# Four norms and the final one in two token halves, and the conditioning tile moved behind the last up tile

## The chip, the core and the metric

The kernel runs on one core of a Trainium2 chip. Its engines work side by side, each from its own instruction stream, and wait for each other on semaphores: TensorE (PE in the profile, with its weight loads as PEld), VectorE (DVE), ScalarE (ACT), GpSimd (POOL) and SyncE (SP), which issues most DMAs. The metric is the time of the whole program on the device in microseconds (us).

## The reference

Two transformer stacks of two layers each run one behind the other on 512 tokens of 1024 channels, in float32. What matters here is the shape of a layer (first stack; the second has the same frame, its mixer has other parts, and its first layer also carries 256 context tokens):

```python
cond = jax.nn.silu(c)
for layer in range(DEPTH):
    mod = (cond @ ada_w[layer] + ada_b[layer])[:, None, :]
    shift_m, scale_m, gate_m, shift_f, scale_f, gate_f = jnp.split(mod, 6, axis=-1)
    h = rmsnorm(x, norm_mix_g[layer]) * (1.0 + scale_m) + shift_m
    mixed = attention_head_groups(...) if layer % 2 == 0 else gated_deltanet(...)   # ends in @ w_out
    x = x + gate_m * mixed
    h = rmsnorm(x, norm_ffn_g[layer]) * (1.0 + scale_f) + shift_f
    x = x + gate_f * swiglu(h, ffn_w_in[layer], ffn_w_out[layer])
return rmsnorm(x, final_norm_g)
```

`swiglu` is silu(h @ gate) * (h @ up), then @ down, with 2816 hidden channels. The conditioning of the second stack has one vector for its tokens and one for its context.

## The kernel before

Activations lie as [128 channels, 8 chunks, tokens]: `X` holds the residual stream. Layers are 0 to 3. Each large product is made of three passes over rounded operands: every operand is split in a high part (rounded by ScalarE) and a low part (the rest, by a subtraction), and `pe_three` or `pe_three_pair` multiply high by high, high by low and low by high. Weights come in tiles through a ring of four slots (`ring`), in the order of `linear_plan()`; ScalarE rounds a tile (`round_tile`, 128x2048, L386), GpSimd or, for the context's passes, VectorE makes the low part (`rest_tile`, L398), two buffers in turn. A projection's tile is "own" if TensorE multiplies it.

The feed-forward part goes in two halves of the hidden channels: `up{layer}{pass}{half}` with 11 own tiles (48 matmuls of 512 columns each), then `down...` with 8 tiles (33 matmuls each), which VectorE adds to `X` with the gate (L794). Beside the up tiles of layers 0 to 2 lie the tiles of the next layer's conditioning matrix ("ada" tiles), one behind each own tile. VectorE multiplies such a tile by the conditioning vector, chunk after chunk in a chain of its own (`dve_ada_tile`, L916 and L919: eight operations for one vector, sixteen for two), and TensorE adds up the partitions with matmuls of one column (`pe_ada_tile`, L935). There are two vectors beside up100, up101 and up200, one beside up000, up001 and up201. A twelfth ada tile per half, `after_down...`, stands behind the down tiles: VectorE works on it at the seventh down tile, TensorE behind the eighth. `dve_ada_end` then forms the modulation (`MOD`, `GAIN`).

Norms: `act_square` squares each chunk of `X` (ScalarE), `pool_add` sums the chunks (GpSimd, L824), `pe_norm_sum` sums over partitions with a matrix of ones (L836), `act_rstd` makes the reciprocal root by Ln and Exp (L842, L843). Then chunk by chunk VectorE scales (`dve_scaled_chunk`, L870), ScalarE adds the shift and rounds to `H_HI` (L857), and VectorE makes `H_LO` (`dve_rest_chunk`, L877), on which TensorE waits chunk by chunk (`wait_normed`). In front of up000, up100 and up300 this follows an output projection of four tiles (`pe_out`, `dve_out`, `act_out`, `pool_out`; an out tile also has 48 matmuls; its residual add is L611), in front of gdn_in and of the final norm it follows a down projection. The first tile of gdn_in is split in halves `U_HI`, `U_LO` behind the norm's Exp (`round_halves`, L1875, and L1890).

The order on each engine is its program order:

```python
def dve_split_norm(dve, name, gain, shift):
    dve.wait_ge(sig("norm_rstd"), RSTD_NO[name])
    dve_scaled_chunk(dve, NORMED, 0, T, gain, 0)
    dve_scaled_chunk(dve, NORMED, 0, T, gain, 1)
    for k in range(DC):
        if k + 2 < DC:
            dve_scaled_chunk(dve, NORMED, 0, T, gain, k + 2)
        dve_rest_chunk(dve, NORMED, T, shift, k)
```

## Time and profile before

| | |
|---|---|
| runs | 3418.53 us median of 3 (3416.69 to 3419.86) |
| profiled execution | 3420.76 us, span 3419.0 us |
| TensorE | busy 3194.0 us, 93% of the span |
| VectorE, ScalarE, GpSimd | 49%, 35%, 38% |
| mean granted TensorE clock | 0.974 |

The span runs from the first to the last instruction. A row of a timeline gives start, duration, engine, line, operation, output and inputs, how many alike are merged (x3), and in brackets how long the engine had been idle and what released it. PEclk is the granted clock of TensorE: 1.00 is 2.4 GHz, 0.50 is 1.2 GHz.

### The profile page before, as it was taken

The numbers are of one execution on the slowest core, as the hardware profiler recorded it, in microseconds if no ns is written. First come the engines' busy times: TensorE is split into PE (matmuls) and PEld (weight loads), VectorE is DVE, ScalarE is ACT, GpSimd is POOL, SyncE is SP. The second block draws the span as 40 slices with busy tenths as digits, with TensorE's granted clock in tenths as the row PEclk, the third lists the DMA queues.
The fourth block names the chain that finished last, engine by engine and source line by source line (L and its number), as shares of the span: only waits on it lengthen the run. The fifth ranks groups of instructions, "written<-read, shape, count | busy, mean of one in ns | idle before, by whom it ended". The sixth has DMA issues, their size and how long they took to land. (4 is left out here: it accounts for less than half of the span.)

```text
span 3419.0 us, 42414 instructions
## 1 busy us (share of the span) xinstructions
PE 3194.0 (93%) x16184; PEld 2510.1 (73%) x16184; DVE 1674.1 (49%) x2845; ACT 1180.5 (35%) x1519; POOL 1315.1 (38%) x719
## 2 busy tenths in 40 slices
PE   8998999998988899998988998999999997989998
PEld 7864788877768688886873367888899783378887
DVE  5534342426676574754836626634355738421111
ACT  3244322224744322223234432222444324432222
POOL 3314444344452433343315543344400424554443
PEclk9999999999999899999998999999999998999999
DMA  7510343432200243442110022444454211022321
GB/s 276 206 41 25 111 185 141 181 132 74 74 13 14 98 172 141 162 152 74 62 48 34 1 78 107 164 154 169 146 180 160 87 50 44 25 86 83 111 84 67
DMA packets 55219, 360.10 MB, mean 105 GB/s; under 512 B 5920, under 2 KB 6944, under 8 KB 19616
## 3 DMA queue, kind: packets, MB, share of 16 engines
q1 hardware_dynamic: 54208, 348.63, 27.8%
q10 hardware_dynamic: 864, 9.44, 0.7%
q8 instruction: 100, 1.64, 0.2%
q14 instruction: 47, 0.39, 0.0%
HBM read 355.95 MB, written 2.10 MB: 105 GB/s over the span
## 5 line engine op out<-in xcount | busy, mean ns | idle before, releaser
L398 POOL TENSOR_TENSOR W_LO<-ring,W_HI 128x2048 fp32r<-128x2048 f32 (+1 forms) x177 | 728.9, 4118 | 1052.5 <-ACT W_HI L386 1052.5
L454 PE MATMUL PS<-H_HI,W_HI 128*128 128x512 f32 (+1 forms) x1888 | 712.5, 377 | 29.7 <-DVE H_LO L877 23.0
L456 PE MATMUL PS<-H_HI,W_LO 128*128 128x512 f32 (+1 forms) x1888 | 703.0, 372 | 0.0
L455 PE MATMUL PS<-H_LO,W_HI 128*128 128x512 f32 (+1 forms) x1888 | 702.4, 372 | 0.0
L386 ACT ACTIVATE W_HI<-ring 128x2048 fp32r<-128x2048 f32 (+1 forms) x214 | 366.3, 1712 | 458.7 <-PE PS L444 417.8
L454 PEld LDWEIGHTS PS<-H_HI,W_HI 128*128 128x128 f32 x1888 | 359.5, 190 | 93.9 <-issue 32.0
L456 PEld LDWEIGHTS PS<-H_HI,W_LO 128*128 128x128 f32 x1888 | 358.7, 190 | 63.1
L455 PEld LDWEIGHTS PS<-H_LO,W_HI 128*128 128x128 f32 x1888 | 359.5, 190 | 59.2 <-issue 0.2
L919 DVE SCALAR_TENSOR_TENSOR PS<-ring,SC,PS 128x256 f32<-128x256 f32 x774 | 379.1, 490 | 27.2
L442 PE MATMUL PS<-HID_HI,W_HI 128*128 128x512 f32 (+1 forms) x880 | 325.3, 370 | 4.8 <-DVE W_LO L398 4.0
L444 PE MATMUL PS<-HID_HI,W_LO 128*128 128x512 f32 (+1 forms) x880 | 323.8, 368 | 0.0
L443 PE MATMUL PS<-HID_LO,W_HI 128*128 128x512 f32 (+1 forms) x880 | 323.7, 368 | 0.0
L650 ACT ACTIVATE GATED<-PS 128x512 f32<-128x512 f32 (+1 forms) x110 | 61.1, 555 | 725.0 <-PE PS L456 725.0
L665 DVE TENSOR_TENSOR HIDDEN<-GATED,PS 128x512 f32<-128x512 f32 (+1 forms) x110 | 69.7, 634 | 425.0 <-ACT GATED L650 425.0
L794 DVE SCALAR_TENSOR_TENSOR X<-PS,MOD,X 128x512 f32<-128x512 f32 (+1 forms) x80 | 55.7, 696 | 386.0 <-PE PS L444 386.0
L442 PE MATMUL PS<-H_HI,U_HI 128*128 128x512 f32 x520 | 208.3, 401 | 19.8 <-DVE H_LO L877 13.8
L443 PE MATMUL PS<-H_LO,U_HI 128*128 128x512 f32 x520 | 205.0, 394 | 0.0
L444 PE MATMUL PS<-H_HI,U_LO 128*128 128x512 f32 x520 | 204.5, 393 | 0.0
L442 PEld LDWEIGHTS PS<-HID_HI,W_HI 128*128 128x128 f32 x880 | 165.9, 189 | 34.5 <-DVE W_LO L398 5.3
L444 PEld LDWEIGHTS PS<-HID_HI,W_LO 128*128 128x128 f32 x880 | 165.9, 188 | 27.8
L443 PEld LDWEIGHTS PS<-HID_LO,W_HI 128*128 128x128 f32 x880 | 165.9, 189 | 27.0
L2596 POOL TENSOR_TENSOR U_LO<-ring,U_HI 128x1024 fp32r<-128x1024 f32 x40 | 102.5, 2564 | 214.7 <-ACT U_HI L2584 214.7
(401 smaller groups left out, 5315.3 us busy)
## 6 DMA issues: line engine op xcount, KB each, us to landing
ring<-w_tiles SPq DMA_DIRECT2D x271, 1024.0 KB, 4.8
ring<-d_tiles SPq DMA_DIRECT2D x80, 704.0 KB, 4.2
WORK<-bias_tables ACTq DMA_DIRECT2D x4, 1792.0 KB, 9.0
X<-xT SPq DMA_DIRECT2D x1, 2048.0 KB, 16.2
WORK<-rope_tables ACTq DMA_DIRECT2D x2, 1024.0 KB, 4.9
outT<-H SPq DMA_DIRECT2D x8, 256.0 KB, 2.2
X<-ctxT SPq DMA_DIRECT2D x1, 1024.0 KB, 9.0
CN<-consts SPq DMA_DIRECT2D x1, 835.0 KB, 7.2
```

What stands on the lines that cost most here:

```text
L386: act.activation(W_HI[:, b, 0:w], ring[:, g % SLOTS, 0:w], ACT.Copy).then_inc(sig("tile_rounded"), 1)
L398: eng.tensor_tensor(W_LO[:, b, 0:w], ring[:, g % SLOTS, 0:w], W_HI[:, b, 0:w].bitcast(F32), ALU.subtract).then_inc(sig("tile_split"), 1)
L442: pe.matmul(PS[:, o:o + w], hi(k), x_hi(k), start=k == 0, stop=False)
L443: pe.matmul(PS[:, o:o + w], hi(k), x_lo(k), start=False, stop=False)
L444: mm = pe.matmul(PS[:, o:o + w], lo(k), x_hi(k), start=False, stop=k == n - 1)
L454: pe.matmul(to, hi[:, cols(k, j)], x_hi(k), start=k == 0, stop=False)
L455: pe.matmul(to, hi[:, cols(k, j)], x_lo(k), start=False, stop=False)
L456: mm = pe.matmul(to, lo[:, cols(k, j)], x_hi(k), start=False, stop=k == n - 1)
L650: act.activation(GATED[:, v, 0:w], PS[:, v * 1024:v * 1024 + w], ACT.Silu).then_inc(sig("gate_silu"), 1)
L665: dve.tensor_tensor(HIDDEN[:, v, 0:w], GATED[:, v, 0:w], PS[:, v * 1024 + 512:v * 1024 + 512 + w], ALU.mult).then_inc(evac_done, 1)
L919: ins = dve.scalar_tensor_tensor(out=out, in0=w, scalar=c[:, k:k + 1], in1=acc, op0=ALU.mult, op1=ALU.add)
L2596: pool.tensor_tensor(U_LO[:, i % 2, :].rearrange("p (k c) -> p k c", k=DC), half_source(layer, t, j), U_HI[:, i % 2, :].rearrange("p (k c) ...
```

## The change

1. The norms in front of up000, gdn_in, up100 and up300 and the final norm work on two halves of the tokens (columns 0 to 255, 256 to 511). The last out tile (or last down tile) multiplies the first half for all its outputs, then the second; residual add, square, sum and reciprocal root of the last chunks are made per half. TensorE's sum of the first half lies inside the second half's matmuls, that of the second inside the first pair of the next projection (`pe_first_pair`), which is multiplied half by half.
2. In the up norms ScalarE rounds the second weight tile in four pieces (`round_second`) beside the second half's first chunks, and VectorE makes its low part in four pieces behind its last ones (`rest_second`). GpSimd, which made it before, waits for it.
3. In the last out tile ScalarE squares the tile before ahead of rounding the next weight tile, and GpSimd adds the squares ahead of the low part.
4. For gdn_in the first half weight tile is rounded in front of the norm's first half, the second inside it (`round_early`); the two halves lie in buffers of their own.
5. The twelfth conditioning tile is called `last_up...` and stands behind the last up tile. VectorE works on it behind the low part of the last hidden chunk; TensorE multiplies it inside the first down tile, in front of the last chunk. `dve_ada_end` comes at the third down tile.
6. The result is stored in pairs of chunks and token halves.

```diff
                     plan.append((up, "w", UP if layer == 3 else 2 * UP, UP, 1, None))
+                    if layer < 3:
+                        plan.append((f"last_{up}", "w", 1, 0, 1, None))
                     plan.append((down, "d", DC, DC, 1, None))
-                    if layer < 3:
-                        plan.append((f"after_{down}", "w", 1, 0, 1, None))
...
+        def pe_first_pair(pe, o, hi, lo, normed, between, ends, lag=(0, 0), second=None):
+            for h in range(2):
+                for s in range(DC + lag[h]):
+                    for j in range(2):
+                        k = s - lag[h] * j
+                        if not 0 <= k < DC:
+                            continue
+                        if j == 0:
+                            normed(h * DC + k)
+                        if j and k == h == 0 and second:
+                            second()
+                        to, x_hi, x_lo = PS[:, o + j * 512 + h * HALF:o + j * 512 + (h + 1) * HALF], H_HI[:, k, columns(h)], H_LO[:, k, columns(h)]
+                        pe.matmul(to, hi(j, k), x_hi, start=k == 0, stop=False)
+                        pe.matmul(to, hi(j, k), x_lo, start=False, stop=False)
+                        mm = pe.matmul(to, lo(j, k), x_hi, start=False, stop=k == DC - 1)
+                        if h and k == DC - 1 and ends[j] is not None:
+                            mm.then_inc(ends[j], 1)
+                    if h == 0 and s == 1:
+                        between()
...
+            b_p = base("act", "part_added", 2)
+            for j in range(2):
+                act.wait_ge(sig("part_added"), b_p + j + 1)
+                act_square(act, norm, 6 + j, 0, T)
+            act_rstd(act, norm, OUT_SUM, 0, T, chain, 0)
+            act_part(act, 0, 0, shift)
+            act_part(act, 0, 1, shift)
+            act.wait_ge(sig("out_first_added"), b + OWN[name])
+            act_square(act, norm, 8, 0, T)
+            for k in range(2, 5):
+                act_part(act, 0, k, shift)
+            act.wait_ge(evac_done, E0[name] + OWN[name])
+            act_square(act, norm, 9, 0, T)
+            act_part(act, 0, 5, shift)
+            act_part(act, 0, 6, shift)
+            act_rstd(act, norm, OUT_SUM, 0, T, chain, 1)
+            act_part(act, 0, 7, shift)
+            for k in range(DC):
+                if k < PIECES:
+                    round_second(act, norm, k)
+                act_part(act, 1, k, shift)
+            act.activation(SM[:, 45:46], SM[:, 1:2], ACT.Silu)
...
+            if halves:
+                next_own(pool, name, rest_tile, OWN[name] - 1, OWN[name] - 1, 0)
+                pool_add(pool, NEXT[name], DC, width)
...
+        def dve_norm_parts(dve, norm, gain, shift, between):
+            for h in range(2):
+                dve.wait_ge(sig("norm_rstd"), RSTD_NO[norm] - 1 + h)
+                for s in range(DC + 1):
+                    if s < DC:
+                        dve_part_scaled(dve, h, s, gain)
+                    if h == 0 and s + 1 in between:
+                        between[s + 1]()
+                    if s:
+                        dve_part_rest(dve, h, s - 1, shift)
+                    if h and s >= DC + 1 - PIECES and norm.startswith("up"):
+                        rest_second(dve, norm, s - (DC + 1 - PIECES))
...
                 dve.tensor_tensor(HID_LO[:, bass.ds(m, 1), 0:w], HIDDEN[:, v:v + 1, 0:w],
                                   HID_HI[:, bass.ds(m, 1), 0:w].bitcast(F32), ALU.subtract).then_inc(sig("hidden_split"), 1)
+                if "last_" + name in G0 and isinstance(m, int) and m == UP - 1:
+                    dve_ada_tile(dve, layer + 1, "last_" + name, int(name[-1]) * (UP + 1) + UP, 0, 0, 1, chain, apart=3)
...
+            def wait_first(k):
+                if k == UP - 1 and last in G0:
+                    pe_ada_tile(pe, layer + 1, int(name[-1]) * (UP + 1) + UP, 1, not closes(name))
+                wait_hidden(k)
...
                 next_own(dve, name, rest_tile, m, u, i)
-                if after in G0 and isinstance(m, int) and m == DC - 2:
-
-                    dve_ada_tile(dve, layer + 1, after, int(name[-1]) * (UP + 1) + UP, 0, 0, 1, chain)
...
+            shift = MOD[:, 1, 0:DC, 0]
+            for k in range(4):
+                act_part(act, 0, k, shift)
+            act.wait_ge(evac_done, E0[name] + DC)
+            act_square(act, norm, DC, 0, T)
+            round_early(act, 1)
+            act_part(act, 0, 4, shift)
+            act_part(act, 0, 5, shift)
+            act_rstd(act, norm, PART_SUM, 0, T, chain, 1)
...
+                    pe_first_pair(pe, 0, lambda j, k: U_HI[:, j, k * P:(k + 1) * P], lambda j, k: U_LO[:, j, k * P:(k + 1) * P],
+                                  normed, lambda: pe_norm_sum(pe, "gdn_in", PART_SUM, T, 1), (sig("half_done"), tile_done),
+                                  (4, 6), lambda: pe.wait_ge(sig("half_split"), 2))
...
-        def dve_out_norm(dve):
-            dve.wait_ge(sig("norm_rstd"), RSTD_NO["out"])
-            for k in range(DC):
-                dve.scalar_tensor_tensor(out=H[:, k, 0:T], in0=X[:, k, 0:T], scalar=FIN_G[1][:, k, 0:1],
-                                         in1=NORM_RSTD[:, 0:T], op0=ALU.mult, op1=ALU.mult).then_inc(sig("out_normed"), 1)
+        def dve_out_norm(dve, add_second):
+            for h in range(2):
+                dve.wait_ge(sig("norm_rstd"), RSTD_NO["out"] - 1 + h)
+                for k in range(DC):
+                    if h == 0 and k == 5:
+                        add_second()
+                    dve.scalar_tensor_tensor(out=H[:, k, columns(h)], in0=X[:, k, columns(h)], scalar=FIN_G[1][:, k, 0:1],
+                                             in1=NORM_RSTD[:, columns(h)], op0=ALU.mult, op1=ALU.mult).then_inc(sig("out_normed"), 1)
```

## Rows read from the trace of the kernel before

**Rows 1.** TensorE's waits: the row of the up projections' matmuls.

```profile
PE PS L454 <- DVE H_LO L877: 23.0, 5, 5.3
```

**Rows 2.** Timeline, norm before up300: start us, us, engine, line, operation.

```profile
3035.90 0.75 DVE L611 SCALAR_TENSOR_TENSOR X<-PS,MOD,X 128x512 f32<-128x512 f32 x1 [4.69 <-PE PS L444]
...
3039.91 2.08 DVE L870 SCALAR_TENSOR_TENSOR NORMED<-X,GAIN,NORM_RSTD 128x512 f32<-128x512 f32 x3 [3.26 <-ACT NORM_RSTD L843]
...
3042.79 0.47 PE L454 MATMUL PS<-H_HI,W_HI 128*128 128x512 f32 x1 [4.31 <-DVE H_LO L877]
...
3048.53 2.07 DVE L877 SCALAR_TENSOR_TENSOR H_LO<-NORMED,MOD,H_HI 128x512 fp32r<-128x512 f32 x3
...
3052.78 4.56 POOL L398 TENSOR_TENSOR W_LO<-ring,W_HI 128x2048 fp32r<-128x2048 f32 x1 [16.96 <-ACT W_HI L386]
...
3057.58 0.47 PE L454 MATMUL PS<-H_HI,W_HI 128*128 128x512 f32 x1 [2.03 <-POOL W_LO L398]
```

**Rows 3.** Windows, TensorE alone: busy time, instructions, granted clock.

```profile
core 0: us, PE busy (x), PEclk, DMA share, GB/s
370.00:380.00 10.00, 10.00 (x46) 1.00 0.19 62
2502.00:2507.00 5.00, 5.00 (x44) 1.00 0.42 144
1197.70:1203.50 5.80, 5.80 (x15) 0.51 0.75 280
3042.80:3048.00 5.20, 5.20 (x16) 0.67 0.00 0
3057.50:3063.50 6.00, 5.92 (x26) 1.00 0.49 175
```

**Rows 4.** Timeline, VectorE, the context's norm before layer 2.

```profile
1605.34 1.27 DVE L877 SCALAR_TENSOR_TENSOR CTX_LO<-BIG,MOD,CTX_HI 128x256 fp32r<-128x256 f32 x3
```

**Rows 5.** Timeline, norm before up000.

```profile
381.78 0.75 DVE L611 SCALAR_TENSOR_TENSOR X<-PS,MOD,X 128x512 f32<-128x512 f32 x1 [4.69 <-PE PS L444]
...
403.49 0.47 PE L454 MATMUL PS<-H_HI,W_HI 128*128 128x512 f32 x1 [0.60 <-POOL W_LO L398]
```

**Rows 6.** Timeline, norm before gdn_in.

```profile
763.49 0.75 DVE L794 SCALAR_TENSOR_TENSOR X<-PS,MOD,X 128x512 f32<-128x512 f32 x1 [6.73 <-PE PS L444]
...
768.49 5.47 POOL L1890 TENSOR_TENSOR U_LO<-ring,U_HI 128x1024 fp32r<-128x1024 f32 x2 [9.70 <-ACT U_HI L1875]
...
771.68 2.83 DVE L877 SCALAR_TENSOR_TENSOR H_LO<-NORMED,MOD,H_HI 128x512 fp32r<-128x512 f32 x1
...
774.65 0.77 PE L442 MATMUL PS<-H_HI,U_HI 128*128 128x512 f32 x1 [8.58 <-DVE H_LO L877]
...
784.78 2.40 POOL L1890 TENSOR_TENSOR U_LO<-ring,U_HI 128x1024 fp32r<-128x1024 f32 x1 [10.81 <-ACT U_HI L1885]
```

**Rows 7.** Timeline, up100's first conditioning tile.

```profile
1187.79 0.48 DVE L916 TENSOR_SCALAR PS<-ring,SC 128x256 f32<-128x256 f32 x1
...
1196.29 1.62 PE L935 MATMUL PS<-SM,ACC 128*128 128x1 f32 x8 [3.71 <-DVE ACC L919]
...
1197.77 0.77 PE L454 MATMUL PS<-H_HI,W_HI 128*128 128x512 f32 x1
```

**Rows 8.** Timeline, VectorE, the final norm.

```profile
3406.95 0.75 DVE L794 SCALAR_TENSOR_TENSOR X<-PS,MOD,X 128x512 f32<-128x512 f32 x1 [6.73 <-PE PS L444]
...
3410.96 5.39 DVE L1115 SCALAR_TENSOR_TENSOR H<-X,PR,NORM_RSTD 128x512 f32<-128x512 f32 x8 [3.26 <-ACT NORM_RSTD L843]
```

**Rows 9.** Timeline, VectorE, end of up100 and first down tile.

```profile
1308.96 0.69 DVE L668 TENSOR_TENSOR HID_LO<-HIDDEN,HID_HI 128x512 f32 x1 [0.95 <-ACT HID_HI L652]
...
1309.57 0.48 DVE L916 TENSOR_SCALAR PS<-ring,SC 128x256 f32<-128x256 f32 x1
...
1320.46 0.69 DVE L668 TENSOR_TENSOR HID_LO<-HIDDEN,HID_HI 128x512 fp32r<-128x512 f32 x1 [0.70 <-ACT HID_HI L652]
...
1326.88 0.75 DVE L794 SCALAR_TENSOR_TENSOR X<-PS,MOD,X 128x512 f32<-128x512 f32 x1 [5.73 <-PE PS L444]
```

More of the change, by code:

```diff
@@ L407, in over_own @@
             apart = SLOTS // per
-            rounds = (n - 1) // per
-            base = chain.n if chain else 0
+            rounds = (n - 1 - first) // per
             def step(m, v, i):
@@ L414, in step @@
                 body(m, v * apart, i)
+            for m in range(first):
+                step(m, m, 0)
+            base = chain.n if chain else 0
             if rounds:
@@ L554, in act_out @@
-            act_rstd(act, OUT_SUM, 0, width, chain)
+            if not in_halves_norm(norm):
+                squares(OWN[name] - 1)
+                act_rstd(act, norm, OUT_SUM, 0, width, chain)
+                return
+            b_p = base("act", "part_added", 2)
+            for j in range(2):
+                act.wait_ge(sig("part_added"), b_p + j + 1)
+                act_square(act, norm, 6 + j, 0, T)
+            act_rstd(act, norm, OUT_SUM, 0, T, chain, 0)
+            act_part(act, 0, 0, shift)
@@ L601, in dve_out @@
             b = base("dve", "out_first_done", OWN[name])
-            for m in range(OWN[name]):
+            for m in range(OWN[name] - halves):
                 for j in range(2):
@@ L816, in pool_add, with add @@
-        def pool_add(pool, k, w):
+                if m == 2 and last in G0:
+                    dve_ada_end(dve, layer + 1, last, chain)
+            if not halves:
+                dve_beside(dve, layer, name, DC - 1)
+                return
+            b_p = base("dve", "part_done", 1)
+            def add(h):
+                if h:
+                    dve.wait_ge(tile_done, g0 + DC)
+                else:
+                    dve.wait_ge(sig("part_done"), b_p + 1)
+                o = down_part(h)
+                dve.scalar_tensor_tensor(out=X[:, DC - 1, columns(h)], in0=PS[:, o:o + HALF], scalar=gate[:, DC - 1:DC],
+                                         in1=X[:, DC - 1, columns(h)], op0=ALU.mult, op1=ALU.add).then_inc(
+                    evac_done if h else sig("part_added"), 1)
@@ new lines, in dve_down, with in_halves_norm @@
+            add(0)
+            if norm == "out":
+                dve_out_norm(dve, lambda: add(1))
+            else:
+                dve_norm_parts(dve, norm, GAIN[:, 1, 0, :, 0], MOD[:, 1, 0:DC, 0], {4: lambda: add(1)})
+        CLOSED = {"down001": "gdn_in", "down101": "block", "down201": "in3", "down211": "in3_ctx", "down301": "out"}
+        IN_HALVES_NORM = {"up000": 2, "gdn_in": 1, "up100": 2, "up300": 2, "out": 1}
+        def in_halves_norm(norm):
+            return norm in IN_HALVES_NORM
@@ new lines, in square_units, with added_units @@
+        def square_units(norm):
+            cut = DC - IN_HALVES_NORM[norm] if norm in IN_HALVES_NORM else DC
+            return [(k, None) for k in range(cut)] + [(k, h) for h in range(2) for k in range(cut, DC)]
+        def added_units(norm):
+            return [n for n, (k, _) in enumerate(square_units(norm)) if 0 < k < DC - 1]
+        SQUARED_NO, ADDED_NO, SUMMED_NO, RSTD_NO = {}, {}, {}, {}
+        _at = [0, 0, 0, 0]
+        for _norm in ["attn_in", "up000", "gdn_in", "up100", "block", "in2", "up200", "in3", "in3_ctx", "up300", "out"]:
+            SQUARED_NO[_norm], ADDED_NO[_norm], SUMMED_NO[_norm] = _at[:3]
+            _parts = 2 if in_halves_norm(_norm) else 1
+            if _norm != "in2":
+                _at = [_at[0] + len(square_units(_norm)), _at[1] + len(added_units(_norm)), _at[2] + _parts, _at[3]]
+            _at[3] += _parts
+            RSTD_NO[_norm] = _at[3]
@@ L843, in act_rstd @@
             act.activation(r, r, ACT.Exp, scale=-0.5).then_inc(sig("norm_rstd"), 1)
-        RSTD_NO = {name: n + 1 for n, name in enumerate(
-            ["attn_in", "up000", "gdn_in", "up100", "block", "in2", "up200", "in3", "in3_ctx", "up300", "out"])}
         def act_split_norm(act, w, shift, silu=True):
```

364 lines of the change are left out of this document (257 added, 107 removed).

## The prediction

> **What bounds the kernel now.** I read the page first: TensorE is busy for 93% of the span, no other engine for more than half of it (the table above), so a change pays only where it takes away time in which TensorE waits or works slowly, and costs wherever it makes TensorE wait. Then TensorE's waits: the row at the top for the up projections names the low part of the normalised activations, 23.0 us in five waits [rows 1]. These waits are the ends of norms. Then the timeline around each of the five norms that the change halves, and the granted clock behind each stall.
>
> The norm in front of up300 shows the pattern [rows 2]. VectorE's last residual add (3035.90) follows the last matmul of the out projection by 0.2 us. Then sum of squares, Ln and Exp, and VectorE starts to scale at 3039.91; TensorE starts at 3042.79. VectorE's 16 operations end at 3050.60 (3048.53 and 2.07). Only then is the second weight tile rounded, GpSimd makes its low part from 3052.78 to 3057.34, and the second tile starts at 3057.58 after 2.03 us of waiting: 21.9 us after the out projection's last matmul (3035.70), for one tile of 48 matmuls. A tile costs 10.9 us at 0.227 us a matmul (46 in 10.00 us, less the overlap at the edges) [rows 3]. So nearly 9 us are lost here, two of them to a slow clock: behind the 4.31 us stall the clock is 1.2 GHz for some us. Granted clock in the rows: 0.67 over the 5.20 us behind that stall, 0.51 over 5.80 us from 1197.7, behind a stall of 3.71 us that comes up below, and 1.00 behind the one of 2.03 us [rows 3]. So 3.4 us (twice 0.33 of 5.20) to 5.7 us (twice 0.49 of 5.80) went at 1.2 GHz in place of 2.4, and half of it is lost: 1.7 to 2.9 us; I take 1.9 us.
>
> **The norm in front of an up projection, in halves (three places).** I count from the start of the last out tile, 10.9 us before its end; in this count VectorE now starts at 15.1, ends at 25.7, and the second tile starts at 32.8 [rows 2]. Matmuls of 256 columns follow each other by 0.1195 us (44 in 5.00 us, less the edges) [rows 3]; two make 0.239 us against 0.227 for one of 512, so halving costs 0.6 us a tile, and 4.8 us over the 402 matmuls halved (three out tiles, four first pairs, two down tiles). These are in the counts below. New order: first token half of the last tile done at 5.7, twelve matmuls of the other to 7.2, and the first half's add and square are done by then. The path from the add's start through square, sum, Ln and Exp to VectorE is 4.0 us now (3039.91 less 3035.90); what of it lies behind the square, at half width, I estimate at 2.2 us. VectorE starts at 9.4, 5.7 us sooner. A half operation repeats every 0.395 us (three from 1605.34 take 1.27, the last of them 0.48 on its own) [rows 4], so 32 take 12.6 us, where 16 whole ones take 10.6. It also gets two late residual adds (0.8) and four 512-wide pieces of the second weight tile's low part (such operations repeat every 0.66 us, 10.6 over 16; I take 0.6 for a plain subtraction): 15.9 us. Waits inside, all estimates: GpSimd's half add up to 0.7; the second half's Exp, which ScalarE takes behind parts 5 and 6, 0.9; and in the second half ScalarE rounds a 512-wide piece beside each of the first four chunks, 0.6 and 0.4 if it is as fast as VectorE by width, against VectorE's 0.79, so up to 1.0 more. VectorE ends at 28.1, **2.4 us later than now**. TensorE starts the first pair at 12.5, waits 0.9 for the last square, and ends with VectorE at 28.3. The wait is from the pieces: without inner waits VectorE ends at 25.3, with them doubled at 30.7. These are the bounds.
> - **up300** has no conditioning tiles. Second tile at 28.4 for 32.8: **-4.4 us** (-7.3 to -2).
> - **up000** has. VectorE makes the first conditioning tile behind the norm, and TensorE must multiply it before the second weight tile. Now this is hidden: second tile at 403.49, 21.9 us behind the last matmul's end (0.2 before 381.78), after 0.60 us for the weights [rows 5]. New: 28.1 and half of 8.3 (one vector) and 0.5: 32.8, the same; but TensorE has now stood for 4.2 us, so the clock falls: **+2.0 us** (-0.6 to +4.5).
> - **up100** has two vectors: 16 VectorE operations from 1187.79 until TensorE's 1196.29, 8.3 us of work and a little; TensorE already waits 3.71 us for them, and its second tile starts at 1197.77, 35.7 in this count, slow [rows 7]. VectorE 2.4 us later moves it by as much: **+2.3 us** (-0.4 to +4.8).
>
> **The norm in front of gdn_in.** The last residual add is at 763.49; GpSimd makes both low parts of the first weight tile from 768.49, 5.47 us, and VectorE's operation at 771.68 takes 2.83 us in place of 0.75; TensorE starts at 774.65, and the second weight tile is ready at 787.18 [rows 6]. From the last down tile's start (755.8) that is 31.5. New: first half of the tile to 4.0, twelve matmuls and sum to 6.5, VectorE from 7.5. The first low part comes before the norm; the second is made from 12.1 on, and holds VectorE by what the row at 771.68 shows, 2.83 less 0.75: 2.1 us. Chunk 4 is there at 15.1, TensorE waits 2.3 us for it, rest of the pair paced by VectorE to 23.5, then the trailing chunks, 27 matmuls: pair done at 26.7; the second tile's low part (2.40 us of GpSimd, started by the pair's first half at 23.9) is ready at 27.6: **-3.9 us** (-6, if nothing is held, to 0, if the clock falls in the pair and both holds are long).
>
> Here a rule of the Trainium skill bears on the case: SBUF — State Buffer, section "SBUF: two separate sides", says that a VectorE operation with two SBUF inputs and a GpSimd operation exclude each other for a whole instruction. By it the hold is all of GpSimd's operation, half of 5.47 us, and the pair ends 0.5 us later. The trace agrees (2.83 us at 771.68), and the sum above does not use it.
>
> **The final norm.** Add at 3406.95, eight operations from 3410.96 for 5.39 us, then the last store [rows 8]. From the last down tile's start (3399.3) VectorE now ends at 17.1. New: second half's reciprocal root at 12.8, eight half operations 3.2: 16.0. **-1.0 us** (-2 to +1: the stores have half as long runs, and nothing here shows their rate).
>
> **The conditioning tile behind the last up tile.** This is the largest term. Now VectorE makes it at the seventh down tile and TensorE multiplies it behind the eighth; neither waits. New: VectorE starts it behind the last low part of the hidden activations, and TensorE multiplies it inside the first down tile, before its last chunk. In order: that low part starts at 1320.46, and on the tile before VectorE's next operation starts 0.6 us after it (1309.57 after 1308.96), so 1321.1 here [rows 9]. Two vectors take 8.3 us, as above: ready at 1329.4. TensorE's last matmul of the first down tile ends 0.2 us before the add at 1326.88, and the last three start 0.7 before that: 1325.9 [rows 9]. It stands 3.5 to 3.6 us, with all eight down tiles queued in order behind it. Then eight tiny matmuls, and the clock falls, as at 1196.29 after 3.71 us: 1.9. **+5.5 us**, at each place with two vectors: behind up100, up101 and up200: **+16.5 us** (10.5 if the clock holds, 21 if each slow stretch is the longest). With one vector VectorE is ready at 1325.3 of this clock, some 0.3 us before TensorE asks (up000, up001, up201): 0. The multiplication itself only moves. The loads of the ring move by a slot; the first down tile's load is then released by the conditioning multiplication 11 us before its use, and rounding and low part (a larger tile's takes 4.56 us) still fit behind the load: 0, and about 1 us if they don't. SP's queue has nothing else behind it.
>
> Squares ahead of the next split, and the added order of waits, lie inside the last out tile beside TensorE's work: in the count above, 0 of their own.
>
> **Sum.** -4.4 + 2.0 + 2.3 - 3.9 - 1.0 + 16.5 = +11.5 us. The profiled execution took 3420.76 us, its span 3419.0; the median of the runs is 3418.53, 2.2 us below. From the median: **3430.0 us**.
>
> **Rivals.**
> - *No stall at the conditioning tile* (VectorE is ready by another order of its work than I read, so 16.5 falls to 0). For it: VectorE is idle half of the time on average. Against: the operations are a chain in program order, and up100 shows the same stall at 3.71 us. 3418.5 - 5.0 = 3413.5, no change by a hair. 0.08.
> - *Faster*: the stall as above is gone, or stays with the clock up (10.5), and the inner waits of the four half norms are absent, so that they stand at their low bounds: -7.3 - 0.6 - 0.4 - 6 - 2 = -16.3. With 10.5: 3412.7. It decides where VectorE needs no more than 15.9 us at an up norm. 0.10.
> - *Norms as computed or better, the stall short*: two of three stalls without a clock fall and up norms 1.5 us better each: about +2, 3421. 0.12.
> - *The hold of VectorE by GpSimd reaches the up norms.* GpSimd's low part of the first up tile (4.56 us) must now follow the first-half add and ends at 9.4, just as VectorE starts. 1 to 2 us late in each, and the clock falls in a first pair that stutters: +7 more, 3437. For it: the margin is nil. 0.12.
> - My forecast, its own range 3424 to 3436: 0.58.
>
> **Numbers.** Range: 3415 to 3439 leaves out some of the fast and of the slow rivals' tails. A measurement of this kernel tells some 0.2% (6.8 us) from no change. Slower by more (over 3425.4): 0.58 and 0.12, less a tail, 0.68. Within: 0.12, 0.08 and a hundredth of the forecast's: 0.21. Faster: 0.10 and a hundredth: 0.11.
>
> **What would show each step.** TensorE's waits: three rows at the conditioning multiplication of about 3.6 us inside the first down tiles of up100, up101, up200, and granted clock of half behind them. At up100 its wait for the conditioning tile grows from 3.7 to about 8 us; at up000 a new one of 4 us. The waits for the activations' low part shrink from 4.3 us to below 1 in the up norms, and at gdn_in to about 2.3. The spacing of halved matmuls stays 0.12 us. The prediction is wrong if VectorE ends an up norm near 25 in my count, or if its conditioning chain is ready before TensorE asks.

## The result and the profile after

The changed kernel took 3442.02 us (median of 4 runs, 3437.23 to 3444.36), the one before on the same chip 3419.2 us (4 runs, 3416.69 to 3424.51). The ratio is 1.0056, 95% interval 1.0044 to 1.0068: 19 us slower (15 to 23). Forecast were 3430.0 us, range 3415 to 3439, and slower with 0.68; so the sign is right and the size short by 8 us against the ratio. The profiled execution took 3444.36 us, span 3442.3, mean granted clock 0.967 (before 0.974); it is the slowest of the four, so its trace shows 23 us of loss where the ratio of the medians shows 19.

TensorE's waits after the change; the numbers behind a row are us in total, times, longest:

```profile
PE PS L1238 <- DVE ACC L1222: 36.4, 8, 11.2
...
PE PS L464 <- DVE H_LO L1180: 11.8, 2, 7.1
...
PE PS L497 <- DVE H_LO L774: 4.8, 9, 1.8
```

The waits for the activations' low part were 23.0 us in five [rows 1]. Of these two are left (11.8), in the whole norms at the very start (7.1, where it was 5.3) and before up200 (4.7); the three of 4.31 us in front of up000, up100 and up300 are gone, and small ones stand in the halved first pairs (L497). But the conditioning multiplication (L1238) waits 36.4 us in eight; before, it was 17.3 us in three. Of these 19 us, 9.9 are three new stalls at the moved tile, 3.7 a new one at up000, 4.2 the growth of the one at up100, and 1.3 small ones elsewhere. So the waits for the norms went down as forecast, and more came up on another row.

Timeline of the changed kernel at the end of up100 and the first tile of down100, VectorE and TensorE together (compare [rows 9]):

```profile
1322.16 0.69 DVE L852 TENSOR_TENSOR HID_LO<-HIDDEN,HID_HI 128x512 fp32r<-128x512 f32 x1 [0.70 <-ACT HID_HI L836]
1322.76 0.48 DVE L1219 TENSOR_SCALAR PS<-ring,SC 128x256 f32<-128x256 f32 x1
...
1327.47 0.39 PE L454 MATMUL PS<-HID_HI,W_LO 128*128 128x512 f32 x1
...
1330.63 0.48 DVE L1222 SCALAR_TENSOR_TENSOR ACC<-ring,SC,PS 128x256 f32<-128x256 f32 x1
...
1331.16 1.70 PE L1238 MATMUL PS<-SM,ACC 128*128 128x1 f32 x8 [3.31 <-DVE ACC L1222]
1332.72 0.77 PE L452 MATMUL PS<-HID_HI,W_HI 128*128 128x512 f32 x1
...
1334.38 0.75 DVE L1050 SCALAR_TENSOR_TENSOR X<-PS,MOD,X 128x512 f32<-128x512 f32 x1 [3.28 <-PE PS L454]
...
1343.78 0.75 DVE L1050 SCALAR_TENSOR_TENSOR X<-PS,MOD,X 128x512 f32<-128x512 f32 x1 [8.64 <-PE PS L454]
```

Read it from the bottom of the chain: the last of VectorE's sixteen operations ends at 1331.11, 8.35 us after the first began, and TensorE, which had stopped behind 1327.47, goes on at 1331.16. That is the predicted stall, 3.31 us for 3.5 to 3.6. The same row stands at 1529.05 (3.31) and 2239.09 (3.30), behind up101 and up200. Then the clock, in windows of TensorE alone (busy, matmuls, granted clock, DMA share, GB/s):

```profile
1320.00:1330.00 10.00, 7.86 (x39) 1.00 0.20 72
1331.00:1334.00 3.00, 2.84 (x11) 0.56 0.09 15
1334.00:1338.00 4.00, 4.00 (x11) 0.50 0.95 363
1338.00:1342.00 4.00, 4.00 (x19) 0.97 0.87 301
```

What a stretch loses is its length times what the clock lacks of 1.00: 0.44 of 3.00, 0.50 of 4.00, 0.03 of 4.00, together 3.4 us. The prediction had 1.9. Over the 8.00 us from 1529.00 and from 2239.00 the clock is 0.57 too, which gives 3.4 us each.

The conditioning waits at up000 and up100, the norm before gdn_in, and the norm before up300:

```profile
404.06 1.02 PE L1238 MATMUL PS<-SM,ACC 128*128 128x1 f32 x4 [3.69 <-DVE ACC L1222]
...
774.42 0.39 PE L497 MATMUL PS<-H_HI,U_PARTS 128*128 128x256 f32 x1 [1.83 <-DVE H_LO L774]
...
788.43 0.47 PE L452 MATMUL PS<-H_HI,U_PARTS 128*128 128x512 f32 x1 [1.53 <-POOL U_PARTS L2189]
...
1197.31 1.87 PE L1238 MATMUL PS<-SM,ACC 128*128 128x1 f32 x8 [7.88 <-DVE ACC L1222]
...
3054.96 0.28 PE L528 MATMUL PS<-O_HI,W_HI 128*128 128x256 f32 x1
...
3064.17 0.88 DVE L767 SCALAR_TENSOR_TENSOR HIDDEN<-X,GAIN,NORM_RSTD 128x256 f32<-128x256 f32 x2 [2.77 <-ACT NORM_RSTD L1150]
...
3081.41 0.69 DVE L659 TENSOR_TENSOR W_LO<-ring,W_HI 128x512 fp32r<-128x512 f32 x1
...
3082.36 0.40 PE L464 MATMUL PS<-H_HI,W_HI 128*128 128x512 f32 x1
```

At up300, counted from the last out tile's start (3054.96), VectorE starts at 9.2 (forecast 9.4), ends at 27.1 (28.1), and the second tile starts at 27.4 (28.4) where it was 32.8.

**Where the time went, stage by stage.** VectorE's residual adds mark the stages. The table gives the us from the first add of one projection to the first add of the next (to the end of the span in the last column), from the timelines of one profiled execution each; stages that never differ by more than 0.2 us are left out. The experiments' kernels are described below.

| kernel | out0 to down000 | down001 to out1 | out1 to down100 | to down101 | to out2 | out2 to down200 | to down201 | to down210 | down211 to out3 | out3 to down300 | down301 to end |
|---|---|---|---|---|---|---|---|---|---|---|---|
| before | 176.9 | 429.3 | 186.8 | 191.0 | 491.0 | 206.7 | 186.0 | 127.4 | 373.1 | 173.4 | 65.3 |
| act_peel | 176.9 | 430.2 | 185.1 | 191.0 | 494.6 | 206.8 | 186.1 | 124.6 | 375.4 | 173.4 | 65.3 |
| cond_only | 177.5 | 430.1 | 190.5 | 197.6 | 496.3 | 212.7 | 186.8 | 124.2 | 372.9 | 173.5 | 65.3 |
| **after** | 179.1 | 424.9 | 194.5 | 197.8 | 495.6 | 214.5 | 187.5 | 124.2 | 378.1 | 168.0 | 63.9 |
| filler | 179.3 | 428.3 | 191.6 | 194.6 | 494.9 | 211.5 | 185.6 | 124.2 | 379.8 | 168.0 | 64.0 |
| cond_short | 179.2 | 424.9 | 191.1 | 194.2 | 495.5 | 210.0 | 186.6 | 124.2 | 371.8 | 167.9 | 63.9 |
| cond_back | 179.3 | 428.2 | 187.3 | 191.1 | 496.0 | 207.1 | 186.5 | 124.2 | 379.9 | 168.0 | 63.9 |
| first_short | 177.5 | 423.9 | 185.8 | 191.1 | 494.1 | 208.7 | 186.5 | 124.2 | 378.0 | 168.0 | 64.0 |
| fill_first | 176.4 | 424.0 | 186.6 | 191.1 | 496.2 | 207.1 | 186.5 | 124.3 | 379.9 | 168.0 | 63.9 |
| up100_on | 177.5 | 423.2 | 188.2 | 191.0 | 494.8 | 206.7 | 186.5 | 124.2 | 376.6 | 167.9 | 64.0 |
| back_three | 177.5 | 423.2 | 185.2 | 190.9 | 494.6 | 206.8 | 186.5 | 124.2 | 380.1 | 167.9 | 63.9 |
| up300_off | 177.5 | 423.4 | 185.2 | 190.9 | 494.6 | 206.7 | 186.5 | 124.2 | 380.1 | 173.5 | 64.0 |

The columns of **after** add up to 21 us over before; the rest of the 23 us between the two spans is the stretch ahead of the first add (350.2 against 348.2).

### The profile page after: what moved, and what is told of

The parts are those of the page before. It is cut to its first block and busy times, and to the rows that moved or that the text cites. A ratio compares the mean times of both kernels' runs of the same rounds, so it can differ in the third digit from the quotient of the medians.

```text
span 3442.3 us, 43356 instructions
## 1 busy us (share of the span) xinstructions
PE 3217.5 (93%) x16606; PEld 2549.4 (74%) x16606; DVE 1702.1 (49%) x2937; ACT 1188.4 (35%) x1575; POOL 1301.5 (38%) x719
## 5 line engine op out<-in xcount | busy, mean ns | idle before, releaser
L406 POOL TENSOR_TENSOR W_LO<-ring,W_HI 128x2048 fp32r<-128x2048 f32 (+1 forms) x174 | 715.0, 4109 | 1075.2 <-ACT W_HI L394 1075.2
L464 PE MATMUL PS<-H_HI,W_HI 128*128 128x512 f32 (+1 forms) x1840 | 692.9, 377 | 13.0 <-DVE H_LO L1180 11.8
L466 PE MATMUL PS<-H_HI,W_LO 128*128 128x512 f32 (+1 forms) x1840 | 683.2, 371 | 0.0
L465 PE MATMUL PS<-H_LO,W_HI 128*128 128x512 f32 (+1 forms) x1840 | 683.2, 371 | 0.0
L464 PEld LDWEIGHTS PS<-H_HI,W_HI 128*128 128x128 f32 x1840 | 349.5, 190 | 72.3 <-issue 14.5
L466 PEld LDWEIGHTS PS<-H_HI,W_LO 128*128 128x128 f32 x1840 | 349.4, 190 | 61.0
L465 PEld LDWEIGHTS PS<-H_LO,W_HI 128*128 128x128 f32 x1840 | 349.9, 190 | 57.5 <-issue 0.2
L452 PE MATMUL PS<-H_HI,U_PARTS 128*128 128x512 f32 x504 | 202.6, 402 | 10.5 <-POOL U_PARTS L2189 5.6
L453 PE MATMUL PS<-H_LO,U_PARTS 128*128 128x512 f32 x504 | 199.5, 396 | 0.0
L454 PE MATMUL PS<-H_HI,U_PARTS 128*128 128x512 f32 x504 | 199.1, 395 | 0.0
L2901 POOL TENSOR_TENSOR U_PARTS<-ring,U_PARTS 128x1024 fp32r<-128x1024 f32 x40 | 102.6, 2566 | 217.1 <-ACT U_PARTS L2889 217.1
L454 PEld LDWEIGHTS PS<-HID_HI,W_LO 128*128 128x128 f32 x858 | 163.5, 191 | 27.6
```

The costliest lines, as they stand in the source:

```text
L406: eng.tensor_tensor(W_LO[:, b, 0:w], ring[:, g % SLOTS, 0:w], W_HI[:, b, 0:w].bitcast(F32), ALU.subtract).then_inc(sig("tile_split"), 1)
L452: pe.matmul(PS[:, o:o + w], hi(k), x_hi(k), start=k == 0, stop=False)
L453: pe.matmul(PS[:, o:o + w], hi(k), x_lo(k), start=False, stop=False)
L454: mm = pe.matmul(PS[:, o:o + w], lo(k), x_hi(k), start=False, stop=k == n - 1)
L464: pe.matmul(to, hi[:, cols(k, j)], x_hi(k), start=k == 0, stop=False)
L465: pe.matmul(to, hi[:, cols(k, j)], x_lo(k), start=False, stop=False)
```

## The experiments

Theory A: the loss is the conditioning tile with two vectors in the first down tile, by its stall and by the clock that falls behind it; the halved norms are a small gain in sum. Theory B: the loss comes from the halving itself (narrow matmuls, more instructions). Theory C: as A, but a stall costs only its length. Ratios are to the kernel before, which ran beside each. Where two ratios are compared, the difference carries some 5 us of uncertainty.

**cond_only.** Before, with the conditioning tile moved (part 5 of the change), and with the loops over own tiles (ScalarE's, and TensorE's in some down projections) in the changed form, that is, with their first step ahead of the loop:

```diff
+                    if layer < 3:
+                        plan.append((f"last_{up}", "w", 1, 0, 1, None))
                     plan.append((down, "d", DC, DC, 1, None))
-                    if layer < 3:
-                        plan.append((f"after_{down}", "w", 1, 0, 1, None))
```

> The kernel before with one part of the change alone: the conditioning tiles that stood behind the down tiles are made behind the last up tile and multiplied inside the first down tile; norms whole, as before. Theory A (the loss is here: at the three places with two vectors TensorE stands for VectorE's 16 operations, and its clock falls behind each): three waits of 3.3 us at the conditioning multiplication inside the first tiles of down100, down101 and down200, the stretch behind each at a lower granted clock, about 6.7 us a place, +20 us against before (3439). Theory B (the loss comes from the halved norms with their narrow matmuls and extra instructions, and the conditioning tile only moves): within 3 us of before. Theory C (the stalls cost only their length): +10 us.

Measured: 3442.94 us against 3423.18, ratio 1.0057 (1.0043 to 1.0072). That is 20 us (15 to 25) over before, with no norm halved; theory B falls. Theory C's +10 lies outside the interval, but the new form of the loops is in this kernel too, and alone it measured +3 us (0 to 6, act_peel below); the test of C by itself is filler. The three stalls are 3.31, 3.30 and 3.31 us. The slow stretch is not the same behind each: the granted clock is 0.57 over 8.00 us from 1328.50 and 0.79 over 8.00 us from 1526.30, so 3.4 and 1.7 us are lost there.

**cond_back.** The changed kernel, with the tiles of two vectors where they were:

```diff
-                    if layer < 3:
+                    one = layer == 0 or (layer == 2 and half == 1)
+                    if layer < 3 and one:
                         plan.append((f"last_{up}", "w", 1, 0, 1, None))
                     plan.append((down, "d", DC, DC, 1, None))
+                    if layer < 3 and not one:
+                        plan.append((f"after_{down}", "w", 1, 0, 1, None))
```

> The changed kernel with the two-vector conditioning tiles back behind the last down tile; the one-vector ones stay inside the first down tile, and the five norms stay in halves. Theory A: the three stalls of 3.3 us and the slow stretches behind them are gone, -20 us against the changed kernel, and with what the halved norms bring (up300 -5, gdn_in -4.6, final norm -1, up000 +2.3, up100 +3) -4 to -6 us against before: about 3413 to 3415. Theory B: still over 10 us slower than before, for the narrow matmuls and the norms' extra instructions remain. Theory C: -10 us against the changed kernel, about 3428.

Measured: 3422.69 us, ratio 0.9994 (0.9985 to 1.0003). The loss is gone, as A has it; B's 10 us of loss and C's 3428 are not there. But against before the five halved norms bring only 2 us (-5 to +1), not 4 to 6. The table says where it went: in this execution the columns of the two mixers (to out2 and to out3) are 5.0 and 6.8 us longer than before. Part of that comes with the new form of the loops: against act_peel (ratio 1.0009), which has that form and no halved norm, the halves bring some 5 us. I come back to the mixers.

**cond_short.** The changed kernel, with four of the second vector's chunks left out in the moved tile (that part of the modulation is not computed):

```diff
+                    if name.startswith("last_") and v == 1 and 2 <= k < 6:
+                        continue
```

> The changed kernel, in which the second vector of each conditioning tile inside a first down tile leaves out four of its eight row chunks, so that VectorE makes it in 12 operations in place of 16: this part of the modulation is not computed fully. VectorE is then ready 2.1 us sooner (four operations of 0.52 us), and the three stalls shrink from 3.3 to about 1.2 us. Theory A (the fall of the clock behind a long stall is half of the price): the clock stays up behind the short stalls, and each place gives 4 to 5.5 us, -12 to -16 us against the changed kernel. Theory C (the stall costs its length alone): 2.1 us a place, -6 us. Theory B: no change beyond 2 us.

Measured: 3428.03 us, ratio 1.0011 (1.0002 to 1.0020): 15 us less than the changed kernel's ratio, which fits A's 12 to 16 and not C's 6. The stalls are 1.20 us, as expected. That the clock stays up behind them is wrong at the first place:

```profile
1327.99 1.05 PE L1240 MATMUL PS<-SM,ACC 128*128 128x1 f32 x8 [1.20 <-DVE ACC L1224]
```

```profile
1328.00:1331.00 3.00, 3.00 (x16) 0.89 0.30 83
1331.00:1335.00 4.00, 4.00 (x14) 0.65 1.00 408
1335.00:1339.00 4.00, 4.00 (x19) 1.00 0.73 251
```

The wait and the tiny matmuls behind it were followed by a short fall, 1.7 us here (0.11 of 3.00 and 0.35 of 4.00). At down200 it fell again (0.68 over 3.00 us), but behind the same wait of 1.20 us at down101 it stayed up:

```profile
1522.00:1525.00 3.00, 2.87 (x17) 1.00 0.28 45
1525.00:1529.00 4.00, 4.00 (x19) 1.00 0.87 310
```

The table has 3.2 us left of 6.8 (to down101, 194.2 over 191.0, where the changed kernel has 197.8).

**filler.** The changed kernel, with 12 matmuls that nobody reads ahead of the moved multiplication at the three places:

```diff
+                if k == UP - 1 and last in G0 and name in ("down100", "down101", "down200"):
+                    for x in range(12):
+                        pe.matmul(PS[:, 2560:2560 + 512], W_HI[...], HID_HI[:, x % 8, 0:512], start=True, stop=True)
                 if k == UP - 1 and last in G0:
```

> The changed kernel, in which TensorE, ahead of the conditioning multiplication inside the first tiles of down100, down101 and down200, works through 12 extra matmuls of 512 columns whose result nobody reads (12 by 0.227 is 2.7 us), so that of the 3.3 us stall 0.6 are left. VectorE is ready when it was, so the multiplication begins at the same time; only TensorE's clock can change. Theory A (half of each place's price is the clock that falls behind the stall): the granted clock stays at 1.0 behind the multiplication, and each place gives back 2.5 to 3.4 us, -8 to -10 us against the changed kernel (3432 to 3434 where that stands at 3442). Theory C (no part of the price is the clock): no change. Should the tiles behind wait for something else (weights loaded later), the clock stays up and the time stays too.

Measured: 3435.05 us, ratio 1.0029 (1.0019 to 1.0038), 9 us less than the changed kernel's 1.0056; theory A expected 8 to 10, theory C none. Work that serves nothing makes the kernel faster. Timeline and windows of the first place:

```profile
1329.39 2.88 PE L876 MATMUL PS<-HID_HI,W_HI 128*128 128x512 f32 x12
1332.86 1.05 PE L1242 MATMUL PS<-SM,ACC 128*128 128x1 f32 x8 [0.58 <-DVE ACC L1226]
1333.77 0.47 PE L452 MATMUL PS<-HID_HI,W_HI 128*128 128x512 f32 x1
```

```profile
1331.60:1335.00 3.40, 2.82 (x16) 1.00 0.08 10
1335.00:1339.00 4.00, 4.00 (x19) 1.00 0.92 352
```

The clock is 1.00 throughout, the DMA share behind it is as high as in the changed kernel, and the interval to down101 falls from 197.8 to 194.6: of a place's 6.8 us, 3.6 are the stall and what surrounds it, and 3.2 the clock.

**back_three.** cond_back with the norms of up000 and up100 whole:

```diff
-        IN_HALVES_NORM = {"up000": 2, "gdn_in": 1, "up100": 2, "up300": 2, "out": 1}
+        IN_HALVES_NORM = {"gdn_in": 1, "up300": 2, "out": 1}
```

> As the kernel with the two-vector conditioning tiles put back, and besides the norms in front of up000 and up100, whose conditioning tile is what TensorE waits for, whole again; in halves stay those in front of gdn_in and up300 and the final one. Theory A (in those two norms VectorE ends later in halves than whole, and the conditioning operations queue behind it): the stalls of 3.69 us at up000 and the growth from 3.71 to 7.88 us at up100 go, 5.3 us less than with all five in halves, about -11 us against before: 3407 to 3409. Theory B (the halves cost everywhere through narrow matmuls): these two give back only their 0.6 us a tile, about 3 us, and the kernel stays at or above before. This is the version that should beat both kernels if theory A holds.

Measured: 3414.36 us against 3423.18, ratio 0.9971 (0.9960 to 0.9982): 10 us faster than before (11 were expected), 8 faster than cond_back. It beats both kernels. Of these 8 us the trace puts 3.9 at the two norms (1.8 and 2.1); in the two executions compared the rest lies in stretches that these norms don't touch, above all down001 to out1.

**up300_off** (back_three, up300 whole too) and **up100_on** (back_three, up100 in halves too), each by the same dictionary.

> The best kernel so far (two-vector conditioning tiles back; up000 and up100 whole), with the norm in front of up300 whole as well, so that only those of gdn_in and the final one are in halves. As predicted, halving up300 brings 4.4 us; the trace of the changed kernel gives 5. So this one should be 4.5 to 5 us slower than that one: -5 us against before. If the gain of the halves was at gdn_in alone, it stays at -10.

Measured: 3419.72 us, ratio 0.9991 (0.9982 to 1.0000), 7 us slower than back_three by the ratios. The table gives 5.6 us for that column, 173.5 against 167.9, and 0.2 or less in every other.

> The best kernel so far, with up100's norm in halves besides (four norms in halves: up100, gdn_in, up300, the final one). The two of up000 and up100 together cost 8 us in the medians (3422.7 with, 3414.4 without), where the prediction had 4.3. By the prediction's split 2.3 of 4.3 fall to up100; by the traces 3.0 of 5.3. So +3 to +4.5 us against that one, -6 against before. If the loss is at up000 alone, it stays at -10; if all of it is at up100, it comes to -2.

Measured: 3416.93 us, ratio 0.9983 (0.9974 to 0.9992): 4 us slower than back_three, and cond_back 4 slower again. Each of these steps is within the uncertainty of two ratios; that both norms with a conditioning tile behind them lose rests on the table. There it is 3.0 us at up100 (188.2 against 185.2; 187.3 in cond_back) and 1.8 at up000 (179.3 against 177.5).

**first_short.** cond_back, with six of the second vector's operations in up100's conditioning tiles on 8 of 256 columns (that part is not computed):

```diff
+                        if name == "up100" and v and k < DC - 1:
+                            out, w, acc_in = out[:, 0:8], w[:, 0:8], acc[:, 0:8]
```

> The kernel with the two-vector conditioning tiles put back and all five norms in halves, in which the second vector of each of up100's conditioning tiles is computed on 8 of its 256 columns in six of its eight operations (this part of the modulation is not computed). Only the first of these tiles lies on TensorE's path: six operations of 0.52 us shrink to 0.1 to 0.2, so it is ready 1.9 to 2.5 us sooner. Theory A (VectorE's chain behind the norm in halves sets when the second weight tile starts): TensorE's wait of 7.87 us at up100 shrinks by as much, and the kernel is 2 to 3 us faster than with the same norms whole in length. Rival (the second weight tile's low part in pieces, or its load, is late by itself): the wait moves to the next row and less than 1 us is gained.

Measured: 3419.21 us, ratio 0.9988 (0.9979 to 0.9997), about 2 us less than cond_back, which the two medians can't tell from nothing. The wait of 7.87 us shrinks to 6.32, and the interval from out1 to down100 from 187.3 to 185.8, by 1.5 us each: VectorE's chain sets this place, and no second wait takes over.

**fill_first.** cond_back, with matmuls that nobody reads ahead of the first conditioning multiplication, 12 at up000 and 28 at up100:

```diff
                 if first:
                     product(0, 0, 0)
+                    for x in range(12 if name == "up000" else 28):
+                        pe.matmul(PS[:, 2560:2560 + 512], H_HI[:, x % 8, 0:P], H_HI[:, x % 8, 0:512], start=True, stop=True)
                     ada(0, 0)
```

> The kernel with the two-vector conditioning tiles put back and all five norms in halves (3422.7 us), in which TensorE, ahead of the first conditioning multiplication of up000 and of up100, works through 12 and 28 extra matmuls of 512 columns that nobody reads (2.7 and 6.4 us), so that 1.0 of 3.69 and 1.5 of 7.87 us of waiting are left. If the clock that falls behind these stalls is part of what the halves cost there, each place gives back 1.5 to 3 us: -3 to -6 us, 3417 to 3420. If the length of VectorE's chain is all of it, nothing changes, and the clock is up behind the multiplication all the same.

Measured: 3417.04 us, ratio 0.9981 (0.9972 to 0.9990), 4 us less than cond_back. At up000 the clock behind the multiplication is 1.00 where it was 0.50, and the interval falls from 179.3 to 176.4, under the 177.5 of the whole norm. At up100 the clock is only partly kept and 0.7 us come back, less than the 1.5 to 3 expected. Windows behind the multiplication, first of cond_back, then of fill_first, up000 and up100 each:

```profile
404.00:410.00 6.00, 5.81 (x16) 0.50 0.58 218
1201.00:1207.00 6.00, 6.00 (x21) 0.61 0.50 172
```

```profile
401.00:407.00 6.00, 5.06 (x25) 1.00 0.48 162
1192.00:1198.00 6.00, 6.00 (x24) 0.72 0.62 231
```

**act_peel.** Before, with only the form of ScalarE's loops changed:

```diff
-            over_own(act, name, body)
+            over_own(act, name, body, first=1)
...
-            over_own(act, name, lambda m, u, i: next_own(act, name, round_tile, m, u, i))
+            over_own(act, name, lambda m, u, i: next_own(act, name, round_tile, m, u, i), first=1)
```

> The kernel before, in which only ScalarE's loops over the up and down tiles have their first step ahead of the loop, as the change writes them; no conditioning tile is moved and no norm is in halves. In the traces of all kernels that have this form, two waits of TensorE for the low part of a weight tile in the narrow up stage of layer 2 (1.84 and 1.47 us, each behind an ACT_TABLE_LOAD of 1.28 us that stands ahead of a weight tile's rounding) are missing. If the loops' form places these table loads, this kernel loses both waits: -3.3 us, at most the resolution of the medians, but plain in the trace. If they go by the moved conditioning tile, they stay. Likewise for one small VectorE operation in layer 2's mixer that lasts 6.97 us in place of 1.05 in every changed kernel so far: if it comes from VectorE's own changed program, it is absent here, for VectorE's program is the same as before.

Measured: 3424.86 us against 3422.72, ratio 1.0009 (1.0000 to 1.0018). First ScalarE's timeline of before at the narrow up stage of layer 2, then that of act_peel:

```profile
2458.70 1.28 ACT L386 ACT_TABLE_LOAD   x1
2460.00 1.92 ACT L386 ACTIVATE W_HI<-ring 128x2048 fp32r<-128x2048 f32 x1
...
2483.78 1.28 ACT L386 ACT_TABLE_LOAD   x1
2485.07 1.92 ACT L386 ACTIVATE W_HI<-ring 128x2048 fp32r<-128x2048 f32 x1
```

```profile
2462.19 1.91 ACT L386 ACTIVATE W_HI<-ring 128x2048 fp32r<-128x2048 f32 x1
2464.11 1.28 ACT L652 ACT_TABLE_LOAD   x1
```

The loads ahead of the rounding are gone, and with them TensorE's waits of 1.84 and 1.47 us: the interval to down210 falls from 127.4 to 124.6. The loops' form alone does this. But the kernel isn't faster; one reason is a small operation of VectorE in layer 2's mixer. The view of its source line, of before and of act_peel (durations in ns, least, median, most):

```profile
L1442 DVE SCALAR_TENSOR_TENSOR WORK<-WORK,PR x2: 248/650/1053, 1816.6 to 1816.8; 128x4 f32<-128x4 f32 x2
```

```profile
L1444 DVE SCALAR_TENSOR_TENSOR WORK<-WORK,PR x2: 208/3586/6965, 1816.6 to 1823.5; 128x4 f32<-128x4 f32 x2
```

An operation on four columns takes 6.97 us in place of 1.05, and TensorE waits 4.0 us for it; the interval to out2 grows by 3.6. The edit leaves the programs of VectorE, GpSimd, TensorE and SyncE as they are in before, and VectorE's 2845 instructions stand in the same order in both traces, so my expectation that it comes from VectorE's own program is wrong. It lasts as long in every other kernel with the new loops. The table shows two more differences of act_peel that are the clock's. From out1 to down100 it is 1.7 us shorter: TensorE waits 2.8 us for the conditioning tile at up100 in place of 3.7, and the slow stretch behind that wait is half as long. From down211 to out3 it is 2.3 us longer, with a mean granted clock of 0.95 in place of 0.96.

## Why the prediction was right in sign and short in size

**The moved conditioning tile (+16.5 forecast).** Right in place, order and number: three stalls of 3.31, 3.31 and 3.30 us. The term that was mis-sized is the clock, 1.9 us a place. The rows had offered 1.7 to 2.9, and I took a value near the stall of 4.31 us ahead of full matmuls; here tiny matmuls follow the stall, as at up100. That row gave 2.8, and was itself short: its window began 1.2 us after the clock had fallen. In the whole of that stretch, the kernel before lost 3.4 us (0.49 of 7.00):

```profile
1196.50:1203.50 7.00, 7.00 (x22) 0.51 0.62 232
```

Measured in the changed kernel are 3.2 to 3.4. Against kernels with the same loops (act_peel and back_three) the columns of cond_only sum to some 20 us (5.4 to down100, 6.6 to down101, 1.7, 5.9, 0.7). The filler run shows the split. The ratios give 16 us (10 to 22) for the moved tile alone (cond_only less act_peel) and 21 us (16 to 26) beside the halved norms (the changed kernel less cond_back).

**One-vector tiles (0 forecast).** Nearly right: at up001 nothing moves (185.6 us from down000 to down001 in all twelve kernels). The column ahead of down000 grows 0.6 us in the kernels with the moved tile and up000's norm whole (177.5 for 176.9), the one ahead of down201 0.5 in those with the one-vector tiles alone moved (186.5 for 186.0). What these half microseconds are stays open.

**up300 (-4.4).** Right: -5.4. VectorE's 17.9 us came out below the forecast's 18.7: over the 15.9 us of counted work stand 2.0, where the estimate of the inner waits came to 2.8.

**up000 (+2.0) and up100 (+2.3).** Right: +1.8 and +2.1 to +3.0. The new stall at up000 is 3.69 us for 4.2, that of up100 7.88 for 8. fill_first shows that at up000 the loss is the fallen clock and no more; and in first_short the same stall of 3.69 us was followed by 0.72 over 6 us in place of 0.50, and the interval was 177.5, that of the whole norm.

**gdn_in (-3.9).** Right in sign and nearly in size, and the column hides it: against before it shows -4.4 in the changed kernel and in cond_short, -5 to -6 in five others and -1 in two. The norm itself gives the same in all of them. ScalarE reads the second tile's result 85.6 to 85.7 us behind the first add of down001, where before did so at 90.1: -4.5 us. Behind it lies the delta-net mixer, up to out1 337.5 us long in back_three at a mean granted clock of 0.96, 342.6 in cond_back at 0.94, and 339.2 at 0.95 in before: there it varies. The wait inside the first pair is 1.83 us for 2.3. The count was off at both ends: TensorE starts the second tile of before at 788.8, not at 787.18, when its low part is ready, so now was 33.0 and not 31.5; and new is 28.4, not 27.6, with 1.53 us of waiting for the second tile's low part.

**Final norm (-1.0).** Right: -1.4.

**What no term named.** The sum of the norms and of the conditioning tile is +13 to +14 in this profile (+2.2, -4.4, +2 to 3, -5.4, -1.4 and 20). Other things came beside it. The wait and the slow stretch at up100 are 1.7 us shorter, as in act_peel, and the stretch ahead of the first add is 2.0 longer. The table loads went (-3.2). The slow operation of VectorE in layer 2 came (+3.6). And layer 3's mixer took 378.1 us in place of 373.1. With these the sum is +19 to +20 of the profile's 23; the rest is not attributed. In the last the work and the waits at its start are the same, and only the clock differs. The waits and the windows behind down211's end, of before:

```profile
2661.22 0.70 PE L836 MATMUL PS<-NORM_SQ,CN 128*128 128x256 f32 x2 [2.03 <-ACT NORM_SQ L814]
```

```profile
2658.80:2662.80 4.00, 1.10 (x4) 1.00 0.00 0
2662.80:2666.80 4.00, 3.88 (x17) 1.00 0.01 4
```

and of back_three:

```profile
2654.95 0.70 PE L1156 MATMUL PS<-NORM_SQ,CN 128*128 128x256 f32 x2 [2.03 <-ACT NORM_SQ L1130]
```

```profile
2652.50:2656.50 4.00, 1.12 (x4) 0.89 0.01 2
2656.50:2660.50 4.00, 3.85 (x9) 0.50 0.00 0
```

The same wait of 2.03 us, followed by the same wait of 1.00, costs nothing in one kernel and two microseconds and more in the other. Eight of the twelve profiled kernels pay here and further on in this mixer (376.6 to 380.1), four don't or pay half (371.8 to 375.4). So the sum of +11.5 was not wrong by one step alone: its clock term was 4 us short, and of the unnamed effects, -1.7, +2.0, -3.2, +3.6 and about +5, nothing stood in the profile of before that I read. Among the rivals, that GpSimd's hold reaches the up norms (3437) would have given nearly the measured time, but its mechanism did not happen: GpSimd's operation ended at 9.4 in my count, as computed, VectorE had started at 9.2, and its first pair of half operations still took 0.88 us together. The waits in the first pair are of 0.42 us and less.

## What to carry to other kernels

Price a stall of TensorE at its length and the slow stretch behind it, and take that stretch from the row whose surroundings are alike (here, what follows the stall), to its end. Before a chain of one engine is moved into another engine's unbroken run, compare when the chain ends with when it is asked for, with the number of operations at each place: the same move cost 0.6 us or nothing with eight operations and nearly 7 us with sixteen. A trace is one execution: where a column holds a stretch whose clock varies, compare a point closer behind the change. Splitting a norm pays where nothing queues behind it on the engine that does it (up300, gdn_in, the end), and loses where a chain on that engine is what the next tile waits for.

## What the runs showed of the hardware

- Matmuls whose result nobody reads, put in front of a wait, kept the granted clock at 1.00 and were worth 3 us a place, at three waits of 3.3 us and one of 3.69. Ahead of one of 7.87 us, 28 of them left 0.72 over the 6 us behind it and were worth 0.7.
- Of clock and waits: a wait of 1.20 us with eight one-column matmuls behind it was followed by 0.65 over 4 us at one place and by 1.00 at the next, in the same execution; one of 2.03 us was followed by 1.00 in one kernel and by 0.50 over 4 us in another, with the same instructions around it. The length of a wait alone does not tell whether the clock falls.
- Where ScalarE's table loads stand depends on the form of the loop around its operations: 1.28 us each, twice ahead of a weight tile's rounding in before. The Trainium skill gives 1283 ns for a load (ScalarE: Activation LUTs, section "What ACT_TABLE_LOAD costs"), and says that the back end places the loads block by block (ScalarE activation tables: per-element evaluation and per-set limits, section "Table sets in the compiler and the runtime"). The trace agrees with the first (1.28 us) and fits the second: with the first step taken out of the loop the load moves behind the rounding.
- A VectorE operation on four columns lasted 6.97 us in all eleven changed kernels with the new loop form and 1.05 us in before, although VectorE's instructions are the same in act_peel. What holds it stays open: no row of the trace names it.
